# Interleaving four state-space blocks with the attention half of the last output projection, weight slabs cut by rows

## The reference, cut to what matters

```python
attn = nsa_attention(q, kc, vc, k_slc, kv_heads(vsl), k_win, kv_heads(vwn), gates)
attn = attn * jax.nn.silu(z_a)
y = s5_mixer(u, ...)                  # linear state-space recurrence, 32 groups of 16 channels
y = jax.nn.gelu(y)
y = y * jax.nn.sigmoid(y @ glu_w + glu_b)
ssm = y * jax.nn.silu(z_s)
mix = jnp.concatenate([attn, ssm], axis=-1) @ w_out
return x + gate[:, None, :] * mix
```

## Time and profile before

| what | us |
|---|---|
| median of 3 runs | 1947.72 |
| the profiled execution, own device time | 1941.69 |
| its span, first to last instruction | 1939.9 |
| PE busy in the span | 1823.2 |
| DVE busy | 1154.1 |
| ACT busy | 669.9 |

### The profile page before, as it was taken

The page is one execution under the profiler, slowest core; times in us unless marked ns, Lnnn a source line. Parts: engine busy times, 40 slices in busy tenths (PEclk is TensorE's granted clock), DMA queues, the critical chain, the costliest instruction groups (busy, mean ns, idle before and its releaser), DMA issues.

```text
span 1939.9 us, 24528 instructions
## 1 busy us (share of the span) xinstructions
PE 1823.2 (94%) x9449; PEld 1525.6 (79%) x9449; DVE 1154.1 (59%) x2392; ACT 669.9 (35%) x1086; POOL 101.9 (5%) x198
## 2 busy tenths in 40 slices
PE   3999999999999999998999999999999998999669
PEld 3887767988888887777888898888888877777657
DVE  5776565686557656556444448864776587445442
ACT  3323564432232334223232335232323422655120
POOL 0001110000000100110000000010001100000000
PEclk9999999999999999999999999999999999999789
DMA  8444331244533525662222224463436223102501
GB/s 334 142 148 153 105 109 55 104 142 109 204 109 120 183 70 186 226 217 87 87 87 102 73 87 148 141 198 122 145 120 195 98 87 130 44 23 90 204 22 65
DMA packets 44400, 246.00 MB, mean 127 GB/s; under 512 B 6080, under 2 KB 6304, under 8 KB 25728
## 3 DMA queue, kind: packets, MB, share of 16 engines
q1 hardware_dynamic: 23200, 153.26, 22.2%
q0 software_dynamic: 21088, 91.21, 14.2%
HBM read 229.23 MB, written 15.22 MB: 126 GB/s over the span
## 4 chain that ended last, share of the span: by engine, by line
PE 80%; DVE 11%; DMA 4%; ACT 2%; issue 2%; SPq 0%; DVEq 0%; ACTq 0%
PE ps L465 66%; DMA ada_raw<-in_ada 3%; DVE w_lo L1384 3%; PE ps L636 2%; PE ps L657 2%; PE ps L901 2%; PE ps L646 1%; DMA ada_first<-in_ada 1%; DVE ada_raw L1412 1%; PE ps L775 1%; PE ps L882 1%; PE ps L891 1%; ACT w_hi L971 1%; PE ps L939 1%; PE ps L927 1%
## 5 line engine op out<-in xcount | busy, mean ns | idle before, releaser
L1384 DVE TENSOR_TENSOR w_lo<-w_raw,w_hi 128x2048 fp32r<-128x2048 f32 x136 | 311.6, 2291 | 149.4 <-ACT w_hi L971 149.1
L971 ACT ACTIVATE w_hi<-w_raw 128x2048 fp32r<-128x2048 f32 x136 | 260.1, 1913 | 399.3 <-PE ps L465 376.8
L465 PE MATMUL ps<-h_hi,w_hi 128*128 128x512 f32 (+1 forms) x1008 | 379.8, 377 | 14.6 <-issue 5.1
L465 PE MATMUL ps<-h_lo,w_hi 128*128 128x512 f32 (+1 forms) x1008 | 375.0, 372 | 0.0
L465 PE MATMUL ps<-h_hi,w_lo 128*128 128x512 f32 (+1 forms) x1008 | 374.9, 372 | 0.0
L465 PEld LDWEIGHTS ps<-h_hi,w_hi 128*128 128x128 f32 x1008 | 192.7, 191 | 48.4 <-issue 9.3
L465 PEld LDWEIGHTS ps<-h_hi,w_lo 128*128 128x128 f32 x1008 | 192.2, 191 | 32.7
L465 PEld LDWEIGHTS ps<-h_lo,w_hi 128*128 128x128 f32 x1008 | 192.7, 191 | 30.9
L465 PE MATMUL ps<-hid_hi,w_hi 128*128 128x512 f32 (+1 forms) x576 | 211.3, 367 | 0.0
L465 PE MATMUL ps<-hid_hi,w_lo 128*128 128x512 f32 (+1 forms) x576 | 210.6, 366 | 0.0
L465 PE MATMUL ps<-hid_lo,w_hi 128*128 128x512 f32 (+1 forms) x576 | 210.5, 366 | 0.0
(11 more groups left out here) (377 smaller groups left out, 2532.1 us busy)
## 6 DMA issues: line engine op xcount, KB each, us to landing
w_raw<-in_slabs SPq DMA_DIRECT2D x136, 1024.0 KB, 4.8
ada_raw<-in_ada POOLq DMA_DIRECT2D x108, 512.0 KB, 4.5
s_tables<-s_tab POOLq DMA_DIRECT2D x4, 2692.0 KB, 9.5
s_t<-s_tables POOLq DMA_DIRECT2D x4, 2692.0 KB, 9.8
ada_first<-in_ada SPq DMA_DIRECT2D x4, 1536.0 KB, 18.3
a_bias<-in_a_bias POOLq DMA_DIRECT2D x16, 256.0 KB, 3.0
xT<-in_xT SPq DMA_DIRECT2D x1, 2048.0 KB, 20.0
s_toeplitz<-KTp POOLq DMA_DIRECT2D x32, 64.0 KB, 3.3
```

Of the source, the lines that this page charges most:

```text
L465: last = mm(o, l, r, start=start and n == 0, stop=stop and n == 2)
L971: A(w_hi[s][:], w_raw[:, s, :], ACT.Copy).then_inc(sem("hi_done"), 1)
L1384: tt(w_lo[s][:], w_raw[:, s, :], w_hi[s][:].bitcast(F32), ALU.subtract).then_inc(sem("lo_done"), 1)
```

## The change: what it does

The w_out slabs are cut by rows instead of by columns. Slab (16, 0) holds the 4 attention row tiles of the first 4 output tiles, (18, 0) those of the last 4; (16, 1) and (18, 1) hold the 4 state-space row tiles. The order of loading is (16, 0), (18, 0), glu, (16, 1), (18, 1). The 8 attention parts (one output tile each, 4 row tiles, 12 matmuls) are put between the state-space blocks: parts 0 and 1 after `states(1)`, 2 and 3 after `states(2)`, 4 and 5 after `states(3)`, 6 after the outputs of block 3, 7 after the last transposes. Each part is added to the residual by DVE by itself. `states(0)` and the recurrence of block 0 go ahead of the transposes and the gating of step 2. Each block's y tile is transposed, copied and split right after its block (`turn_y`, `turned_y`) instead of all four at the end; the multiplication by `zs` is done there. After glu, two slabs (8 output tiles x 4 row tiles) remain; output tiles are computed in pairs with the row tiles outermost, so that each row tile is waited for by itself. The splits of slabs n = 16 and 17 move behind blocks 0 and 1. `v_a`, `v_b` and `y_lo` move to other places in SBUF. The number of matmuls is unchanged; DVE has one more residual addition for each of the 8 output tiles, and as many multiplications as before.

```diff
-H_SLABS = 0, 1, 2, 3, 4, 13, 6, 7, 14, 9, 10, 5, 8, 11, 12, 15, 16, 17, 18, 19
+H_SLABS = 0, 1, 2, 3, 4, 13, 6, 7, 14, 9, 10, 5, 8, 11, 12, (16, 0), (18, 0), 15, (16, 1), (18, 1)
...
# SP
+                    first, half = slab
+                    sp.dma_start(w_raw[:, n % 2, :].rearrange("p (s c) -> p s c", s=2),
+                                 I["slabs"][S_HQ + first:S_HQ + first + 2, :, D * half:D * half + D].rearrange("s p c -> p s c"))\
...
# PE
-            pe.wait_ge(sem("h_added"), 4)
-            for i in range(4):
-                transposes([h_o[:, t, i * P:(i + 1) * P] for t in range(TT)], "hxo_full")
...
+            def attention_part(o):
+                if o % 4 == 0:
+                    wait(pe, "lo_done", c("slab", 1))
+                b = bank()
+                for k in range(4):
+                    last = product(b, o % 4, k, o_hi, o_lo)
...
+            states(0)
+            pe.wait_ge(sem("h_added"), 4)
+            for i in range(4):
+                transposes([h_o[:, t, i * P:(i + 1) * P] for t in range(TT)], "hxo_full")
+            for blk in range(NBLK):
+                outputs(blk)
                 if blk + 1 < NBLK:
                     states(blk + 1)
+                    if blk == 0:
+                        pe.wait_ge(sem("hx_done"), 4)
+                    attention_part(2 * blk)
+                    attention_part(2 * blk + 1)
+                else:
+                    attention_part(2 * blk)
+                turn_y(blk)
+            attention_part(7)
-            pe.wait_ge(sem("y_lo_done"), 4)
-            slab_t(tile_of(y_hi, y_lo), nk=4, tiles=4)
-            pe.wait_ge(sem("mix_lo"), 4)
-            pe.wait_ge(sem("hx_done"), 4)
-            for _ in range(4):
-                slab_t(mix)
...
# ACT
             for blk in range(NBLK):
                 for q in range(2):
                     act.wait_ge(sem("y_mm"), 2 * blk + q + 1)
...
+                high_y(blk)
+                if blk < 2:
+                    split()
...
# DVE
+            step(V.memset(v_a[:, :, 0:1], 0.0), V.memset(v_b[:, :, 0:1], 0.0))
+            recurrence(0)
+            dve.wait_ge(sem("za_done"), 1)
+            for i in range(5):
...
+            for blk in range(NBLK):
+                y_free(blk)
+                if blk + 1 < NBLK:
+                    recurrence(blk + 1)
+                    attention_part(2 * blk)
+                    attention_part(2 * blk + 1)
+                else:
+                    attention_part(2 * blk)
+                turned_y(blk)
+                if blk < 2:
+                    split()
+            attention_part(7)
             split()
...
-                free(tt(mx_t[:, m % 2, :], sg_t[:, m % 2, :], yT[:, m, :], ALU.mult))
-                freed()
-                tt(mx_t[:, m % 2, :], mx_t[:, m % 2, :], zs[:, m, :], ALU.mult).then_inc(sem("mx_done"), 1)
+                tt(mx_t[:, m % 2, :], sg_t[:, m % 2, :], zs[:, m, :], ALU.mult).then_inc(sem("mx_done"), 1)
```

More of the change, by code:

```diff
@@ L256, in program @@
         y_nat = at("y_nat0", 0, [NCH, 2, L, P]), at("y_nat1", 72 * K, [NCH, 2, L, P])
-        v_a = at("v_a", 42 * K, [P, GB, NCH])
-        v_b = at("v_b", 44 * K, [P, GB, NCH])
+        v_a = at("v_a", 95 * K, [P, GB, NCH])
+        v_b = at("v_b", 97 * K, [P, GB, NCH])
         v_c = at("v_c", 90 * K, [P, GB, NCH])
@@ L265, in program @@
         y_hi = at("y_hi", 80 * K, [P, 4, T], F32R)
-        y_lo = at("y_lo", 32 * K, [P, 4, T], F32R)
+        y_lo = [at(f"y_lo{ct}", o * K, [P, T], F32R) for ct, o in enumerate((42, 44, 70, 103))]
         sg_t = at("sg_t", 24 * K, [P, 2, T])
@@ L369, in _ @@
                 sp.wait_ge(sem("lo_done"), S_HQ + n - 1)
-                sp.dma_start(w_raw[:, n % 2, :], I["slabs"][S_HQ + slab]).then_inc(sem(f"raw_in{n % 2}"), 16)
+                if isinstance(slab, int):
+                    sp.dma_start(w_raw[:, n % 2, :], I["slabs"][S_HQ + slab]).then_inc(sem(f"raw_in{n % 2}"), 16)
+                else:
+                    first, half = slab
+                    sp.dma_start(w_raw[:, n % 2, :].rearrange("p (s c) -> p s c", s=2),
+                                 I["slabs"][S_HQ + first:S_HQ + first + 2, :, D * half:D * half + D].rearrange("s p c -> p s c"))\
+                      .then_inc(sem(f"raw_in{n % 2}"), 16)
             for m in range(KT):
@@ L928, in states, with outputs @@
                     last.then_inc(sem("x_full"), 1)
-            states(0)
-            for blk in range(NBLK):
+            def outputs(blk):
                 t = tables(s5_t[blk % 2])
@@ L942, in _, with product @@
                     last.then_inc(sem("y_mm"), 1)
+            def product(b, m, k, hi, lo):
+                cols, sl = slice(D * (m // 2) + (2 * k + m % 2) * P, D * (m // 2) + (2 * k + m % 2 + 1) * P), c.base("slab") % 2
+                return three(b[:], (w_hi[sl][:, cols], w_lo[sl][:, cols]), (hi[:, k, :], lo[:, k, :]), k == 0, k == 3)
+            def attention_part(o):
[4 more added lines that the diff above has]
+                    last = product(b, o % 4, k, o_hi, o_lo)
+                last.then_inc(sem("slab_used" if o % 4 == 3 else "acc_full"), 1)
+                if o % 4 == 3:
+                    c.add("slab")
@@ L943, in _, with turn_y @@
+            def turn_y(ct):
+                pe.wait_ge(sem("yn_gelu"), 2 * (ct + 1))
+                transposes([y_nat[ct // 2][:, ct % 2, i, :] for i in range(L)], "yt_full")
+            states(0)
[4 more added lines that the diff above has]
+                outputs(blk)
                 if blk + 1 < NBLK:
                     states(blk + 1)
-            for ct in range(4):
-                pe.wait_ge(sem("yn_gelu"), 2 * (ct + 1))
-                transposes([y_nat[ct // 2][:, ct % 2, i, :] for i in range(L)], "yt_full")
@@ new lines, in _ @@
+                    attention_part(2 * blk + 1)
[3 more added lines that the diff above has]
+            attention_part(7)
+            wait(pe, "lo_done", c("slab", 1))
+            for m in range(4):
+                b = bank()
+                for k in range(4):
+                    pe.wait_ge(sem("y_lo_done"), k + 1)
+                    cols = slice((4 * k + m) * P, (4 * k + m + 1) * P)
+                    last = three(b[:], (w_hi[c.base("slab") % 2][:, cols], w_lo[c.base("slab") % 2][:, cols]), (y_hi[:, k, :], y_lo[k][:]),
+                                 k == 0, k == 3)
+                last.then_inc(sem("slab_used" if m == 3 else "acc_full"), 1)
@@ new lines, in _ @@
+            c.add("slab")
+            for slot in range(2):
+                wait(pe, "lo_done", c("slab", 1))
+                for pair in range(2):
+                    bs = bank(), bank()
+                    for k in range(3):
+                        if slot == 0:
+                            pe.wait_ge(sem("mix_lo"), k + 1)
+                        for j in range(2):
+                            product(bs[j], 2 * pair + j, k, h_hi[:, 4:KT, :], h_lo[:, 4:KT, :])
+                    if slot == 0:
+                        pe.wait_ge(sem("mix_lo"), 4)
+                    for j in range(2):
+                        product(bs[j], 2 * pair + j, 3, h_hi[:, 4:KT, :], h_lo[:, 4:KT, :])\
+                          .then_inc(sem("slab_used" if (pair, j) == (1, 1) else "acc_full"), 1)
+                c.add("slab")
@@ L1334, in _ @@
                       accum_out=row_sum[:, s % 8:s % 8 + 1]).then_inc(sem("hp_ready"), 1)
+            c.add("bank", 2)
             for i in range(4):
@@ L1340, in _, with high_y @@
             A(zs[:], zs[:], ACT.Silu).then_inc(sem("zs_done"), 1)
+            def high_y(ct):
+                act.wait_ge(sem("yt_done"), ct + 1)
+                A(y_hi[:, ct, :], yT[:, ct, :], ACT.Copy).then_inc(sem("y_hi_done"), 1)
+                c.add("bank")
             for blk in range(NBLK):
-                c.add("bank", 2)
                 for q in range(2):
@@ L1347, in _ @@
                     c.add("bank")
[L1348 to L1351, removed]
+                if blk + 1 < NBLK:
+                    c.add("bank", 4)
+                else:
+                    c.add("bank")
+                high_y(blk)
+                if blk < 2:
+                    split()
+            c.add("full", 6)
+            c.add("bank")
+            c.add("slab", 2)
             split()
@@ L1360, in _ @@
             c.add("slab")
-            for _ in range(4):
-                skip_t()
+            split()
         @block.vector
@@ L2104, in _, with recurrence @@
             c.add("full", 3)
[L2105 to L2128, removed]
+            def recurrence(blk):
                 t = tables(s5_t[blk % 2])
                 dve.wait_ge(sem(f"tab_in{blk % 2}"), 32 * (blk // 2 + 1))
-                if blk:
-                    y_free(blk - 1)
                 va, vb = v_c[:], wst[:]
@@ L2149, in _, with y_free, attention_part, turned_y @@
                 tt(v_b[:, :, 1:], wst[:, :, 0:NCH - 1], t["Ei"][:, :, 0:NCH - 1], ALU.mult).then_inc(sem("st_done"), 1)
```

(55 more changed lines are left out.)

1 line of the change is left out of this document (removed).

## The result

The changed kernel took 1898.51 us (median of 4 runs, 1895.03 to 1903.35), the kernel before beside it 1947.33 us (4 runs): ratio 0.9754, 95% interval 0.9725 to 0.9782. The profiled execution has a span of 1893.2 us and took 1895.03, 46.7 us less than that of the kernel before (1941.69).

A forecast was written before the change was run, and what follows sets the result against it. PE was taken as the bound, busy 1823.2 of 1939.9 us. Its work in the new order summed to a span of 1898.5, 41.4 less; against the median 1947.72 that gave 1906.3, with an 8 in 10 range of 1901 to 1916.

The forecast's parts named there:

- The walk along PE: PE's new order from the attention's end, priced mostly at full clock: the span ends at 1898.5, 41.4 us less.
- A wait costs twice: On PE behind attention: each wait costs itself and slow work behind it; block 0's outputs lose 3.1 us to the clock.
- The cross-check: Same stretch summed from removed waits (31.1) and clock given back (3 x 3.1, and 1 to 2): 41 to 42 us.
- clock stays low in each block: Rival, chance 0.12: every block's outputs still start slow, giving back 9.3 us of the saving: 1915.6.
- against the median of the runs, 1947.72, I set 1906.3: Whole time: the 41.4 us saving set against the measured median of the kernel before, giving the forecast 1906.3.
- The wait ahead of outputs(0): PE's wait for block 0's recurrence, the one recurrence that nothing covers: 1.8 us.
- The rule of the Trainium skill: Transposes ahead of outputs(0) would not hold the clock up; were it wrong, about 2 us less.
- DVE in time: recurrence(1) ready before PE reaches block 1's outputs, 2.1 us to spare; 2.3 us of slack in later rounds.
- Splits and DMAs moved: Moved splits, table requests and slab loads between the state-space blocks stay hidden: cost 0.
- A late feeder: Rival, chance 0.08: split, Gelu and recurrence share DVE's queue, each round waits 2 to 3.5 us: 1912 to 1915.
- Waits that only move: Rival, chance 0.04: attention parts don't cover the recurrences; only y_lo, h_lo and h_o waits go, 14 to 20 us.
- Slower: Rival, chance 0.02: PE's clock at the low level from 1802 to the end of part 7: 1962.

The follow-up runs named there:

- experiment 7: Changed kernel with all four y tiles turned back, copied and split behind the last attention part: 1909.82 us (2 runs), stretch behind the attention 112.35 us.
- experiment 3: Changed kernel with all eight attention parts moved behind the last state-space block: 1923.53 us, ratio 0.9894, stretch behind the attention 123.7 us.
- experiment 4: Kernel before with 20 extra matmuls, result overwritten, ahead of each of PE's four waits for a recurrence: 1936.15 us, ratio 0.9959, stretch behind the attention 136.6 us.
- experiment 1: Kernel before, unchanged, timed against itself: 1942.66 us (12 runs), ratio 0.9988.
- experiment 8: Changed kernel with 12 extra matmuls in the wait ahead of outputs(0) and ACT's Silu ahead of the gating: 1900.51 us, ratio 0.9768.
- experiment 6: Changed kernel, but the first of the last two slabs waits for all four mix tiles: 1903.24 us (2 runs), stretch behind the attention 108.4 us.

## Why the prediction was right or wrong

**The mechanism: right.** The walk along PE gave 1898.5 - 1794.0 = 104.5 us for the tail; it measured 103.6 and 103.7. By PE's rows the two profiles compare so (us):

| stretch of the tail | before | after | less |
|---|---|---|---|
| from h_q to the first product of outputs(0) | 13.48 | 8.14 | 5.3 |
| outputs(0) | 8.33 | 7.05 | 1.3 |
| waits for v_b ahead of outputs 1 to 3 | 14.4 | 0 | 14.4 |
| outputs 1 to 3 | 22.4 | 16.15 | 6.3 |
| waits for y_lo and h_lo | 12.1 | 0 | 12.1 |
| low clock behind these two, in glu and the projection | 3.7 | 0 | 3.7 |
| all the rest | 71.5 | 72.3 | -0.8 |

The parts, one undone at a time: order of the first block 5.3, interleaving 20.1, y tiles 8.7, mix tiles 4.7, in sum 38.8 of 42.3. They are single removals from the changed kernel and need not add up. The 3.5 us between were not tested; by the table they would be the faster outputs(0) (1.3) and a rest of the y and mix tiles, since experiment 7 still waits for y tile by tile where the kernel before waits for all four. "A wait costs twice" is shown by experiments 3 and 4.

**The cross-check came out by luck.** It had 9.3 us of clock (3 x 3.1) in blocks 1 to 3, "as priced on block 0". But block 0 was the slowest: the others lost 1.4, 2.3 and 2.6, 6.3 in all, and the outputs lose a different amount in each execution (in experiment 1's the four blocks took 6.98, 7.77, 8.17 and 8.20 us). For the start of glu and of the projection it had 1 to 2, where 3.7 were lost, and for outputs(0) nothing, where 1.3 came back. The errors cancel: 11.3 us measured, 10.3 to 11.3 set. The walk along PE doesn't rest on these terms, as it counts all work but the first transposes and outputs(0) at the full clock. The rival "clock stays low in each block" does: its 9.3 would have been some 6.3.

**The step that failed: "against the median of the runs, 1947.72, I set 1906.3", with "2 of scatter".** The saving was taken off a number that was itself high, and the scatter that I allowed was too small. The forecast was 7.8 us too long. Of these, 4.2 are the base: over 23 runs the kernel before has 1943.53, and over 11 others, on another chip, 1943.96, not 1947.72. The saving was 1.5 too small: 42.9 us between 1943.53 and 1900.67, against 41.4. And 2.2 are the four runs of the changed kernel, whose median of 1898.51 lies below the 1900.67 of its second set. With the better base the same saving gives 1902.1, and the range moved along with it (1897 to 1912) holds both 1898.5 and 1900.67.

The 48.8 us of the first comparison are 5.9 more than those 42.9. The profiles place such differences in the stretch in front, not in the work of the change: the unchanged 1790 us took 1789.5 to 1806.1 in ten profiles, while two tails of one program differ by 0.1 (changed) and 0.6 us (before). Why the first runs of the kernel before were the slower ones stays open: only one of them has a profile. Three runs that span 4.9 us were the only sight of this scatter that I had; the range should have been built on that span, not on 2 us.

**The terms.**
- The wait ahead of outputs(0): 1.8 forecast, 2.9 measured. I priced the 16 transposes at 2.82 from the row at low clock; directly behind states(0) they take 1.92, and states(0) 3.6 instead of 3.8. So PE comes 1.1 us earlier and waits that much longer: no difference in the sum.
- Outputs(0): 8.3 taken, 7.05 measured (1797.73 to 1804.78), between the two bounds. The clock fell 1.3 us into them, not at their start. These 1.25 us are more than the 0.9 by which the tail is shorter than forecast; longer rounds take some back.
- The rule of the Trainium skill that a transpose "doesn't count as PE-busy the same way" ("TensorE: Matmul & The Clock Gate", section on PE-mode transpose): by the trace it costs nothing here. The 16 transposes behind states(0) run in 1.92 us at a granted clock of 1.00, and in experiment 8, where they stand in the same place with matmuls behind them instead of a wait, it is 1.00 from 1800 to 1811 us. The wait was what cost.
- DVE in time: right. recurrence(1) ended at 1813.63, PE came at 1814.68: the 2.1 us of slack measured 1.0, as PE needed 1.25 us less for outputs(0). In the next two rounds the slack was 1.5 us where 2.3 was forecast.

```profile
1812.95 0.68 DVE L2188 TENSOR_TENSOR v_b<-wst,s_t 128x504 f32<-128x504 f32 x1
```

- A round: 15.0 forecast, 15.3 measured (outputs 5.38, states 3.6, parts 5.66, turn 0.64); the difference is of the kind priced at 0.8 in all as joints.
- Splits and DMAs moved: nothing on PE's path, as forecast. Of the two slab loads of the tail, that of slab n = 18 took 14.3 us beside block 3's tables, where 4.8 was its price; the other, a half slab too, took 4.8 by itself, as a whole slab did before. The tables of block 3 (Tz) took 13.9 us and were there at 1834.9, before `states(3)` at 1835.34. No PE wait names any of them.
- mix and y: "the 3.8 us wait is gone", "the 8.3 us wait is gone": both, and both come back when undone (experiments 6 and 7).

**The rivals.** Clock low in each block: fallen, every window from 1803 has 1.00. A late feeder: none. Waits that only move: fallen by experiment 3. Slower: no sign of it.

## What to carry to other kernels

Price PE's wait together with the clock behind it: here 4 waits of 4.8 us cost another 9.3 us in the matmuls that followed, and matmuls put into the wait gave that back, useful ones (the attention parts) and useless ones (experiment 4) alike. Price it for each wait by itself: what followed lost between 1.4 and 3.0 us, and not the same in each execution. When a chain of another engine bounds PE, look in the same program for products whose inputs have long been ready, and cut their weights so that they can be taken by themselves. And before a forecast in microseconds is set against a median of three runs, ask how far the unchanged part of the kernel moves between executions: here by up to 16.6 us, against an error of 1.5 us in the saving. To see what a change does, cut both profiles at the last instruction that they share.

## What was not expected of the hardware

The clock is granted differently to the same instructions in different executions: the attention's windows from 1690 to 1710 us were at 1.00 in one execution and at 0.50 in two others, with PE busy 8.1 to 9.9 of 10 us in each. Where h_q started at 1806.1 instead of 1789.6, 10.6 of the 16.5 us arise in this stretch. What decides it, no run here shows.

The end of a 1.6 us wait shows it in small: the 16 transposes behind it took 2.82 us in the profile of the kernel before and 1.97 us in experiment 1, the same program:

```profile
1794.77 1.97 PE L624 MATMUL ps<-ident,h_o 128*128 128x128 f32 x16 [1.64 <-DVE h_o L2101]
```

The tail didn't gain by it. The wait for v_b that follows was 6.5 us instead of 4.8, since DVE's gating and recurrence, and not PE, set when outputs(0) start: 13.48 us behind h_q in one profile and 13.47 in the other.
